# Gate 0's weight rounding between two halves of the normed tiles, keys transposed one gate sooner, query copies and the p block later

## The reference

```python
u = rms_norm(h, kv_norm_w);  k, v = split(u @ kv_w)          # 4 heads of 64 each
k = rope(rms_norm(k, k_norm_w), positions)
u = rms_norm(h, attn_norm_w);  q, gate = split(u @ attn_in_w)  # 1024 and 1024 columns
q = rope(rms_norm(q, q_norm_w), positions)
o = swa_sink_attention(q, k, v, sinks)    # window of 128, blocks of 128 queries
h = h + (o * silu(gate)) @ attn_out_w
h = h + sigmoid(rms_norm(h, w) @ gate_w) * (p_i @ proj_w)     # the "ple" layer
```

## Time and profile before

| | us |
|---|---|
| median of 3 runs | 1391.28 |
| lowest, highest | 1390.82, 1391.56 |
| profiled execution, whole | 1390.0 |
| its span, first to last instruction | 1388.0 |

### The profile page before, as it was taken

How to read it: one execution, slowest core, us unless ns; L and a number is a source line. 1 busy time by engine, 2 the same in 40 slices (tenths; PEclk the granted TensorE clock), 3 DMA queues, 4 the chain that set the end, 5 groups by cost and what they waited for, 6 DMA issues and landing times.

```text
span 1388.0 us, 17862 instructions
## 1 busy us (share of the span) xinstructions
PE 1355.2 (98%) x6632; PEld 1067.7 (77%) x6632; DVE 837.6 (60%) x1439; ACT 680.2 (49%) x1134; POOL 526.9 (38%) x259
## 2 busy tenths in 40 slices
PE   8999999999999999999999999999999999999997
PEld 6877877777788878767888887765667888888886
DVE  5586564757567744785677423468747654544666
ACT  7755635636366533685565312355545333232463
POOL 3453553636220134466000344136523655555200
PEclk9999999999999999999999999999999999999999
DMA  5222313212223233211333233130013233333331
GB/s 191 92 76 61 92 62 91 77 61 78 74 92 94 89 91 92 61 47 47 99 98 122 88 135 96 34 119 15 17 31 91 92 101 97 93 105 92 122 106 61
DMA packets 33220, 117.31 MB, mean 85 GB/s; under 512 B 3948, under 2 KB 4332, under 8 KB 32880
## 3 DMA queue, kind: packets, MB, share of 16 engines
q1 hardware_dynamic: 31976, 111.85, 26.0%
q10 hardware_dynamic: 1160, 4.34, 0.9%
HBM read 114.08 MB, written 2.10 MB: 84 GB/s over the span
## 4 chain that ended last, share of the span: by engine, by line
PE 87%; DVE 5%; ACT 3%; issue 2%; DMA 2%; POOL 1%; ACTq 0%; DVEq 0%
PE bank L1296 84%; PE bank L1750 1%; PE bank L1593 1%; ACT wsh L868 1%; DMA h<-in_xT 1%; DMA arena<-in_alibi 1%; DMA ring<-in_wstream 1%; DVE arena L1911 0%; POOL arena L762 0%; DVE arena L1991 0%; PE bank L1469 0%; POOL wsl L704 0%; PE bank L1504 0%; DVE arena L2283 0%; PE bank L1748 0%
## 5 line engine op out<-in xcount | busy, mean ns | idle before, releaser
L704 POOL TENSOR_TENSOR wsl<-ring,wsh 128x1024 fp32r<-128x1024 f32 x144 | 350.4, 2434 | 556.4 <-ACT wsh L868 556.2
L868 ACT ACTIVATE wsh<-ring 128x1024 fp32r<-128x1024 f32 x199 | 210.3, 1057 | 368.2 <-PE bank L1296 344.6
L1296 PE MATMUL bank<-parts1h,wsh 128*128 128x512 f32 (+1 forms) x736 | 292.0, 397 | 6.0 <-DVE parts1l L1870 1.5
L1296 PE MATMUL bank<-parts1h,wsl 128*128 128x512 f32 (+1 forms) x736 | 285.3, 388 | 0.0
L1296 PE MATMUL bank<-parts1l,wsh 128*128 128x512 f32 (+1 forms) x736 | 285.1, 387 | 0.0
L1296 PE MATMUL bank<-parts0h,wsh 128*128 128x512 f32 x704 | 281.5, 400 | 2.5 <-issue 1.3
L1296 PE MATMUL bank<-parts0h,wsl 128*128 128x512 f32 x704 | 274.5, 390 | 0.0
L1296 PE MATMUL bank<-parts0l,wsh 128*128 128x512 f32 x704 | 274.2, 390 | 0.0
L1296 PEld LDWEIGHTS bank<-parts1h,wsh 128*128 128x128 f32 x736 | 138.2, 188 | 42.7 <-issue 4.1
L1296 PEld LDWEIGHTS bank<-parts0h,wsh 128*128 128x128 f32 x704 | 132.2, 188 | 38.9 <-issue 8.5
L1296 PEld LDWEIGHTS bank<-parts1l,wsh 128*128 128x128 f32 x736 | 138.3, 188 | 28.8 <-issue 2.2
(11 more groups left out here) (320 smaller groups left out, 1802.7 us busy)
## 6 DMA issues: line engine op xcount, KB each, us to landing
ring<-in_wstream SPq DMA_DIRECT2D x206, 512.0 KB, 3.6
arena<-in_alibi ACTq DMA_DIRECT2D x2, 1024.0 KB, 6.4
outT<-arena SPq DMA_DIRECT2D x8, 256.0 KB, 2.8
h<-in_xT SPq DMA_DIRECT2D x2, 256.0 KB, 5.6
h<-in_xT ACTq DMA_DIRECT2D x2, 256.0 KB, 5.9
h<-in_xT SPq DMA_DIRECT2D x1, 512.0 KB, 8.3
h<-in_xT ACTq DMA_DIRECT2D x1, 512.0 KB, 8.6
arena<-in_frow ACTq DMA_DIRECT2D x1, 512.0 KB, 3.3
```

What stands on the lines that cost most here:

```text
L704: return nc.gpsimd.tensor_tensor(dst, src, hi.bitcast(F32), ALU.subtract)
L868: nc.scalar.activation(wsh[n % NSET][:, :], src, ACT.Copy).then_inc(*done("high", ("high", L)))
L1296: return nc.tensor.matmul(*args, **kw)
```

## The change

Three moves in the hand-written list, and one in ACT's code:
- `("hn", "attn")` is cut in two steps of four tiles. kv 2, and with it the rounding of gate 0's weights on ACT and DVE, stands between them; tiles 4 to 7 come after it and before kv 3.
- `("kT",)` moves from behind gate 3 to ahead of the rotation of the first query half, so that TensorE has it between gate 2 and gate 3. The jobs of the keys and of gate 3 change places in the round of banks.
- ACT copies only the first of the four banks of `("qT", 1)` at that step; the other three copies come after the copy of the first unit's transposed probabilities. `("psp", 1)` moves from behind `("qT", 1)` to behind `("aV", 0, 0)`, which on ACT is behind the exponentials of unit (1, 0), on DVE behind the reciprocal of that unit.

No arithmetic is changed.

```diff
--- before.py
+++ after.py
@@ -180,10 +180,10 @@
     for m in range(KD):
         out += [("ple", 0, m)] + (early("kv", m - 1) if m else []) + ([("rope_tables", m // 2)] if m in (1, 3) else [])
     out += early("kv", 7)
-    out += [("kv", 0), ("norm", 2), ("kv", 1), ("nb", 2), ("hn", "attn"), ("kv", 2), ("kv", 3)]
+    out += [("kv", 0), ("norm", 2), ("kv", 1), ("nb", 2), ("hn", "attn", 0), ("kv", 2), ("hn", "attn", 1), ("kv", 3)]
     ro = {s: [("ro", s, t) for t in range(NT)] for s in range(3)}
     out += [("qn", 0), ("gate", 0)] + ro[0] + [("gate", 1)] + [("q", 0, b) for b in range(4)]
-    out += [("qn", 1), ("gate", 2)] + ro[1] + [("gate", 3), ("kT",)] + [("q", 1, b) for b in range(4)]
+    out += [("qn", 1), ("gate", 2), ("kT",)] + ro[1] + [("gate", 3)] + [("q", 1, b) for b in range(4)]
     out += [("qn", 2), ("gate", 4)] + ro[2][:2] + [("gate", 5), ("qT", 0)] + ro[2][2:]
     units = [(n, 2 * G2 + half) for G2 in range(2) for n in range(NT) for half in range(2)]
     swa = pipeline("a", units, [x for x in units if x[1] % 2 == 1])
@@ -196,9 +196,11 @@
             res += [("F", *z) for z in extra] + [y] + extra
         return res
 
-    out += [("gate", 6)] + swa[:7] + [("gate", 7), ("qT", 1), ("psp", 1)]
+    out += [("gate", 6)] + swa[:7] + [("gate", 7), ("qT", 1)]
     between = {u: [("pp", 1, m)] for m, u in enumerate((1, 2, 8, 9))} | {10 + m: [("ao", 0, m)] for m in range(6)}
     body = filled(swa[7:], "a", units, between) + [("ao", 0, 6), ("ao", 0, 7)]
+    k = body.index(("aV", *units[0])) + 1
+    body.insert(k, ("psp", 1))
     k = body.index(("aV", *units[1])) + 1
     out += body[:k] + [("half",)] + body[k:]
     for m in range(KD):
@@ -1085,13 +1087,18 @@
                         nc.scalar.activation(kT[:, :, t * P:(t + 2) * P].rearrange("p a (t b) -> p t a b", t=2),
                                              ps(("kT", t))[:, :].rearrange("p (t a b) -> p t a b", t=2, a=2),
                                              ACT.Copy).then_inc(*done("kT", ("kT", t), ("kT", t + 1), ("free", "kT", t)))
+
+                def turned_query(half, t):
+
+                    key = ("qT", half, t)
+                    act.wait_ge(*at("mm", *key))
+                    nc.scalar.activation(qT[:, 4 * half:4 * half + 4, tok(t)],
+                                         ps(key)[:, :].rearrange("p (a b) -> p a b", a=4), ACT.Copy,
+                                         scale=HD ** -0.5).then_inc(*done("qT", key, ("free", *key)))
+
                 if k == "qT":
-                    for t in range(NT):
-                        key = ("qT", a[0], t)
-                        act.wait_ge(*at("mm", *key))
-                        nc.scalar.activation(qT[:, 4 * a[0]:4 * a[0] + 4, tok(t)],
-                                             ps(key)[:, :].rearrange("p (a b) -> p a b", a=4), ACT.Copy,
-                                             scale=HD ** -0.5).then_inc(*done("qT", key, ("free", *key)))
+                    for t in range(1 if a[0] else NT):
+                        turned_query(a[0], t)
                 if k == "gate":
                     act.wait_ge(*at("mm", *step))
                     if a[0] < KD - 1:
@@ -1121,6 +1128,9 @@
                         act.wait_ge(*at("pv", *AUNIT[u - 2]))
                     nc.scalar.activation(PTb[u % 2][:, 0, :], ps(("aPT", n, g, 0))[:, :], ACT.Copy)\
                         .then_inc(*done("aPT_act", ("aPT", n, g, 0), ("free", "aPT", n, g, 0)))
+                    if u == 0:
+                        for t in range(1, NT):
+                            turned_query(1, t)
                 if k == "aP":
                     n, G2 = a[0], a[1] // 2
                     act.wait_ge(*at("ogf", n, G2))
```

## The result

| | us |
|---|---|
| before, median of 8 runs (lowest, highest) | 1391.41 (1389.89, 1392.74) |
| after, median of 8 runs (lowest, highest) | 1395.64 (1393.27, 1397.15) |
| ratio after to before, 95% interval | 1.0032 (1.0024 to 1.0041) |
| profiled execution after, whole; its span | 1393.27; 1391.4 |
| forecast; its range | 1394.0; 1392.4 to 1396.2 |

The change makes the kernel slower by 0.32%, and the whole interval lies above 0.2%. The time is inside the range, 1.6 us above the forecast, and on the 1395.6 of the rival in which the clock falls. On the direction the prediction was undecided: it gave 0.47 to slower by over 0.2% and 0.49 to a difference within 0.2%. The profiled execution is the shortest of the eight; against the one of before (1390.0) it is 3.3 us longer, and its span 3.4.

The account below looks back on a forecast made before the run. TensorE, busy for 98% of the span, bounds the kernel, so only gaps in its row can move time. The terms 0.68 - 0.18 + 2.25 = +2.75 us, added to the median 1391.28, gave 1394.0 us; range 1392.4 to 1396.2.

Parts of the forecast that it names:

- the rival in which the clock falls: Behind TensorE's 4.1 us idle before the first projection, half clock adds 1.6 us: 1395.6; chance 0.21.
- Part A: Gate 0's rounding after normed tile 3: gate 0 starts 1.48 us earlier, gate 1 0.68 later; costs 0.68 us.
- Part B: Keys' transposes before gate 3: new 0.90 us wait for banks, query block (1, 0) starts sooner; gains 0.18 us.
- Part C: Attention's start: aV (0, 0) starts 1.65 us earlier, but the first projection waits for the p block; costs 2.25 us.
- The rival without exclusion: DVE and POOL don't exclude each other at the p block's low part: Part C costs 1.0, time 1392.8; chance 0.09.
- The sum: Whole kernel: 0.68 - 0.18 + 2.25 = +2.75 us, added to the median; 1394.0 us.
- The rival "nothing takes their place": The stalls at gate 0, query block (1, 0) and aV go without new ones: -4.6 us, 1386.7; chance 0.04.

Follow-up runs that it names:

- A alone: Only the normed tiles' split with gate 0's rounding between the halves, against the kernel before: 1392.26 against 1390.89 us, ratio 1.0010.
- the filled gap: The changed kernel plus four matmuls of ones on constants in the gap before the first projection: 1394.18 us against 1391.11 for the kernel before, ratio 1.0019.
- C alone: Only the later query copies and p block, against the kernel before: 1394.39 against 1390.89 us, ratio 1.0027.
- POOL's added wait: The changed kernel, with POOL's multiplication of unit (1, 0) waiting for the p block's low part: 1394.19 us against 1391.11 for the kernel before, ratio 1.0023.
- eight matmuls: The changed kernel plus eight matmuls of ones on constants before the first projection: 1396.57 us against 1390.89 for the kernel before, ratio 1.0045.
- the p block sooner: The changed kernel with the p block's step behind aT (0, 0) instead of aV (0, 0): 1392.37 us against 1391.11 for the kernel before, ratio 1.0010.
- A made to pay: The kernel before plus the normed tiles' split, with gate 1's low part on DVE ahead of the keys' reductions: 1389.63 against 1391.11 us, ratio 0.9989.
- Silu ahead of the rounding: The kernel before, with ACT reading the bank of gates 3, 6 and 7 before rounding the next weight block: 1389.89 against 1391.49 us, ratio 0.9987.

## Why the prediction came out as it did

**Part A: right, each step within 0.05 us.** Gate 0's low part ends at 485.02 (485.04), gate 1's high part starts at 488.95 (488.99), its low part at 494.24 (494.29), gate 1 at 495.61 (495.66). The profiles of after and of A alone give +0.63 for 0.68. The kernel with the same split and gate 1's low part ahead of the reductions gains, so the loss was that chain, as argued.

**Part B: right.** The transposes start at 528.34, and gate 3 could follow 0.92 later at 529.26; it starts at 530.11, 0.85 late for the forecast 0.90. The 0.57 of the bracket is the part of it that stands as idle time, ahead of the second four. Query block (1, 0) gained 0.15 in after and 0.13 alone, for 0.18; by aS (1, 1) it is 0.25 alone.

**A and B together: a little cheaper than the sum.** 0.48 is left at query block (1, 0), 0.36 at aS (1, 1). Of the 0.12 between, 0.11 comes back in the first matmuls of that query block. In before they stand behind an idle gap and start slowly: the tenth starts 2.15 us after the first (535.21 to 537.36), where after, without a gap, it is 2.04 (535.69 to 537.73). The prediction counted this start for gate 0 and gate 3, but not for the block whose wait goes.

**Part C: the late p block right, the clock wrong.** The high part starts at 590.50 (590.15 by the forecast, and 0.36 of shift from A and B), POOL's multiplication at 591.10, and DVE's low part takes 2.48 us where it takes 1.22 alone: it ends at 594.07, 1.08 after POOL's end at 591.10 + 1.89 = 592.99, as in rows 12 and 13. The projection starts 2.48 later than before counted from aS (1, 1), for the 2.50 of the forecast (593.83 - 591.33), and the 0.23 wait for POOL goes. The forecast put C at 2.25 (its own times, 596.08 - 593.81, give 2.27); the filled gap gives 2.13. The rival without exclusion is refuted: it took an added wait on POOL to see the 1.22, and the 1.26 that this was worth answers to the 593.72 - 592.48 = 1.24 of the forecast. The Trainium skill (SBUF — State Buffer, "SBUF: two separate sides") calls the shared port pair of these two engines an exclusive lock, which the one that comes first, a GpSimd operation or a DVE operation with two SBUF inputs, holds for its whole instruction; the 2.48 against 1.22 agrees.

**The step that was wrong: the clock at full behind the gap.** The sum priced the wait before the projection at its length alone. I took the longest gap of before, 1.62 us, and the fall 2.6 us behind the last work at the end, and gave the clock case 0.21. The gap of 4.09 is well beyond both, and the clock fell in all three profiles that have it or one of 2.83 unfilled. It costs 1.35 in after by the filled gap, 1.4 with POOL's added wait and 1.75 in C alone (11.34 - 9.59), for the 1.6 of the rival. With a gap that long the fall should have been the likeliest case, and the forecast 1395.6. The range held the result only because it was drawn over this rival. The rule of the Trainium skill that the prediction named (TensorE: Matmul & The Clock Gate, "HAM oscillation — how this bites in real kernels") holds here: the clock was at half behind 4.09 us of idleness, and slots were 0.43 us.

**The sum.** In the profiles: 0.36 + 2.13 + 1.35 = 3.84, the figure of the table; 0.42 of it comes back behind aT (1, 0), about 0.24 of it by 923.40 and the rest behind it. The medians differ by 4.2 instead of 3.3. The mean granted clock of the eight runs of after is 0.9954, and that of 23 runs of before in the first experiments 0.9977 (0.9971 for 31 in the next). As an estimate from these, some 0.002 x 2 x 1390 = 5.6 us more stand at half clock. The fall of after lasts 3.4 us (0.37 x 2 x 3 = 2.2 in the window from 593, 1.0 in the next and 0.2 behind it) and costs 1.35, so 5.6 cost about 2.2. With the 2.07 that the waits cost (0.36 + 2.13 - 0.42) that is 4.3, for the measured 4.2. The price per us is taken from one fall and is rough: the fall of C alone lasts 6.8 us and costs 1.75, part of it lying in the wait. The mean clocks put the 5.6 us at the projection's gap: where it stands unfilled (after, C alone, POOL's added wait) the mean clock is 0.9954 to 0.9956, and where it is filled or gone (eight matmuls, four, the p block sooner) 0.9971 to 0.9974, though these three have gate 1's gap as well. That gap shows a fall in one of the six profiles that have it.

**The rival "nothing takes their place"** is refuted by each of the three new stalls. For two of the old stalls it can be had: with A, one edit in DVE's order and one in ACT's, and without B and C, gate 0's and query block (1, 0)'s go without a new one, and the kernel is 4.4 us faster. aV (0, 0)'s stays.

## What to carry to other kernels

When a stall is moved away, find what the releasing engine does next and at what time TensorE will need that: A and C took work off one deadline and put another block of rounding past its own, and B put TensorE's work ahead of the banks that it needs. A gap in TensorE's row of some microseconds can cost more than its length, since the work behind it may run at half clock: here 1.35 us on top of a gap of 4.09. So price a merged gap above the sum of the small ones that it replaces. Where the waiting is for a copy that empties a bank, put the copy ahead of the work that has time, rather than the consumer later.

## What the runs showed of the hardware

- The granted clock fell behind gaps of 4.09 us (twice), 2.83 and 2.24, but not behind the 2.25 of gate 1 in after, nor behind its 2.26 in four other kernels. In the kernel of "A made to pay" it fell even near a gap of 1.61 at aV (0, 0), as its windows show (0.52 is nearly all at half), where before has 1.62 and stays at full. The traces of that kernel and of "Silu ahead of the rounding" have one more each, to half between 919 and 920, behind gaps of 1.14 and 0.68 us, in a stretch that no edit touches and that stays at full in before. Length alone does not decide it. It is probably part of why runs of one kernel differ by 2 to 4 us: of the eight of after, the one with a mean granted clock of 0.997 took 1393.27, and the two with 0.994 took 1395.71 and 1397.15 (though one with 0.996 took 1396.91).

```profile
585.00:588.00 3.00, 1.17 (x10) 0.75 (x11) 0.80 (x2) 3.00 (x6) 1.39 (x1) 1.00 0.01 3
588.00:589.00 1.00, 1.00 (x6) 0.58 (x7) 1.00 (x4) 1.00 (x5) 0.00 (x0) 0.73 0.00 0
589.00:592.00 3.00, 3.00 (x13) 1.84 (x12) 1.70 (x11) 2.95 (x13) 1.28 (x1) 0.52 0.79 242
```

- A plain float32 matmul of 128x512 is recorded as two passes, and takes 0.82 us at full clock (eight in the 6.57 us from 590.98 to 597.55, in the first of the filled gaps), against 0.227 for one of rounded parts.
